# Six tiles between state-space chunks, two of GpSimd's products on ScalarE, and a new order of split weights and attention steps

## What is computed

```python
h = rmsnorm(x, norm_mix_pre[l])
proj = h @ w_in[l]
q_na, k_na, v_na, u_ssm, q_mem = jnp.split(proj, [...], axis=-1)
y_na = neighbourhood_attention(...)          # 8 heads of 128
y_ssm = s5_mixer(u_ssm, ...)                 # complex scan over time, both directions, then gelu and a gate
y_mem = memory_cross_attention(q_mem, mem, mem_norm[l], w_mem_kv[l])   # 4 heads of 128
y = jnp.concatenate([rmsnorm(y_na, ...), rmsnorm(y_ssm, ...), rmsnorm(y_mem, ...)], axis=-1)
x = x + rmsnorm(y @ w_out[l], norm_mix_post[l])
```

```
turns = time * c10 - round(time * c8) + time * c11
```

## Time and profile before

| | |
|---|---|
| median of 3 executions | 2292.43 us (2292.24 to 2294.15) |
| the profiled execution | 2285.35 us, span 2282.8 us |
| mean granted TensorE clock | 0.997 |
| TensorE busy | 2241.6 us, 98% of the span |
| VectorE, ScalarE, GpSimd busy | 1351.2, 1022.7, 120.7 us |

### The profile page before, as it was taken

One profiled execution on the slowest core, in us unless ns is written; L12 is line 12 of the kernel. 1 busy time (PEld: TensorE's weight loads), 2 busy tenths in 40 slices (PEclk: granted clock), 3 DMA queues, 4 the chain that ended last, 5 costly groups with the idle time before them and its releaser, 6 DMA issues.

```text
span 2282.8 us, 32803 instructions
## 1 busy us (share of the span) xinstructions
PE 2241.6 (98%) x13292; PEld 1922.4 (84%) x13292; DVE 1351.2 (59%) x1543; ACT 1022.7 (45%) x1392; POOL 120.7 (5%) x82
## 2 busy tenths in 40 slices
PE   8989999999999999999999999999999999999999
PEld 7878978888888888888888988888888888888887
DVE  6998566565554555454476478757455555445454
ACT  6222465544344444344454467646333344344444
POOL 0674000000000000000000000000000000000000
PEclk9999999999999999999999999999999999999999
DMA  8353435556666655565554433355666665555553
GB/s 319 122 132 128 159 132 210 167 174 187 192 186 194 190 189 197 188 253 189 197 161 141 167 111 94 129 191 162 182 184 184 186 183 198 187 195 191 195 191 111
DMA packets 153352, 402.31 MB, mean 176 GB/s; under 512 B 15264, under 2 KB 30880, under 8 KB 133040
## 3 DMA queue, kind: packets, MB, share of 16 engines
q1 hardware_dynamic: 141952, 394.83, 52.2%
q10 hardware_dynamic: 11312, 6.22, 1.1%
HBM read 398.90 MB, written 2.13 MB: 176 GB/s over the span
## 4 chain that ended last, share of the span: by engine, by line
PE 85%; DVE 4%; ACT 2%; issue 1%; ACTq 0%; DVEq 0%
PE ps L749 20%; PE ps L750 10%; PE ps L787 10%; PE ps L788 10%; PE ps L789 10%; PE ps L989 2%; PE ps L990 2%; PE ps L991 2%; PE ps L624 2%; PE ps L625 2%; PE ps L626 2%; PE ps L616 1%; DVE w_low L2246 1%; PE ps L638 1%; PE ps L639 1%; PE ps L640 1%
## 5 line engine op out<-in xcount | busy, mean ns | idle before, releaser
L2246 DVE TENSOR_TENSOR w_low<-raw_weights,w_high 128x1024 fp32r<-128x1024 f32 (+1 forms) x660 | 777.7, 1219 | 784.0 <-ACT w_high L1473 778.0
L1473 ACT ACTIVATE w_high<-raw_weights 128x1024 fp32r<-128x1024 f32 (+1 forms) x652 | 652.4, 1048 | 800.4 <-PE ps L789 398.5
L749 PE MATMUL ps<-x_split,w_high 128*128 128x512 f32 x2048 | 719.4, 397 | 4.2 <-DVE w_low L2246 2.5
L750 PE MATMUL ps<-x_split,w_low 128*128 128x256 f32 x2048 | 571.6, 279 | 0.0
L749 PEld LDWEIGHTS ps<-x_split,w_high 128*128 128x128 f32 x2048 | 384.4, 188 | 98.4 <-DVE w_low L2246 3.6
L787 PE MATMUL ps<-w_high,x_split 128*128 128x512 f32 x1024 | 398.4, 389 | 0.0
L789 PE MATMUL ps<-w_high,x_split 128*128 128x512 f32 x1024 | 398.4, 389 | 0.0
L788 PE MATMUL ps<-w_low,x_split 128*128 128x512 f32 x1024 | 398.3, 389 | 0.0
L750 PEld LDWEIGHTS ps<-x_split,w_low 128*128 128x128 f32 x2048 | 385.9, 188 | 0.0
L789 PEld LDWEIGHTS ps<-w_high,x_split 128*128 128x128 f32 x1024 | 192.2, 188 | 40.2
L787 PEld LDWEIGHTS ps<-w_high,x_split 128*128 128x128 f32 x1024 | 192.2, 188 | 39.9
(11 more groups left out here) (288 smaller groups left out, 2295.5 us busy)
## 6 DMA issues: line engine op xcount, KB each, us to landing
raw_weights<-in_w_ff SPq DMA_DIRECT2D x128, 1024.0 KB, 5.3
raw_weights<-in_w_up SPq DMA_DIRECT2D x64, 1024.0 KB, 5.6
raw_weights<-in_w_down SPq DMA_DIRECT2D x64, 1024.0 KB, 4.8
raw_weights<-in_w_in SPq DMA_DIRECT2D x62, 1024.0 KB, 5.4
raw_weights<-in_w_out SPq DMA_DIRECT2D x32, 1024.0 KB, 4.9
raw_weights<-in_w_mem_kv SPq DMA_DIRECT2D x7, 1024.0 KB, 14.7
residual<-in_xT SPq DMA_DIRECT2D x2, 2048.0 KB, 14.1
region<-t_table ACTq DMA_DIRECT2D x1, 3072.0 KB, 16.3
```

The lines of the kernel that those rows point to most:

```text
L749: nc.tensor.matmul(o, wh[:, q, w], xs[:, kt], start=(kt == 0), stop=False, skip_group_check=True)
L750: last = nc.tensor.matmul(o[:, 0:S], wl[:, q, w], xh[:, kt], start=False, stop=(kt == KT - 1), skip_group_check=True)
L1473: nc.scalar.activation(split_slot(wh_t, k)[:, r], ring_slot(n)[:, r], ACT.Copy).then_inc(rounded, 1)
L2246: V.tensor_tensor(split_slot(wl_t, k)[:, r], ring_slot(n)[:, r], split_slot(wh_t, k)[:, r].bitcast(f32), ALU.subtract).then_inc(split_read ...
```

## The change

Two columns of products move from GpSimd to ScalarE: `angles(i)` writes time * c8 and time * c11 of chunk i with eight activations of 128 by 128 elements into two pairs of buffers in the `scratch` area (the second buffer of the low parts), and GpSimd keeps five instructions. The chunks stand six tiles apart on TensorE, the last two output products stand in q1, the split of the first q1 slots is woven into VectorE's last chunk, and all attention steps up to unit 10 stand four tiles apart.

```diff
-        PERIOD = 5
+        PERIOD = 6
         BU_AFTER = {2 + PERIOD * i: i for i in range(CHUNKS)}
-        Y_AFTER = {10 + PERIOD * i: i for i in range(CHUNKS)}
-        UNITS_AFTER = {**{67 + 4 * i: i for i in range(7)}, 98: 7, 102: 8, 105: 9, 108: 10}
-        GLU_AFTER, SSM_SUM_AFTER, MEM_SUM_AFTER = 79, 99, 101
+        Y_AFTER = {**{11 + PERIOD * i: i for i in range(CHUNKS - 2)}, 49: CHUNKS - 2, 58: CHUNKS - 1}
+        UNITS_AFTER = {70 + 4 * i: i for i in range(11)}
+        GLU_AFTER, SSM_SUM_AFTER, MEM_SUM_AFTER = 79, 98, 103
...
+            def angles(i):
+                if i >= 2:
+                    act.wait_ge(pool_done, at("turns", i - 2))
+                for part, k in zip(angle[i % 2], (8, 11)):
+                    for j in range(4):
+                        m.did(nc.scalar.activation(part[:, j], iota[:, 0:S:2], ACT.Copy, scale=ssm[k][:, 4 * i + j:4 * i + j + 1]), "angles", i)
...
             tables(2)
+            angles(4)
             na_loads()
             decays(2)
...
             round_slot("q1", 3)
             round_slot("k1", 0)
+            act.wait_ge(dve_done, at("gelu_in"))
+            m.did(nc.scalar.activation(gb, gb, ACT.Tanh, scale=0.7978845608028654), "gelu_tanh")
             act.wait_ge(pool_done, at("na_masked"))
             evac("q1", q1[:, 4:8])
             round_slot("k1", 1)
...
+                whole, fine = angle[i % 2]
+                pool.wait_ge(act_done, at("angles", i))
+                m.did(nc.gpsimd.tensor_scalar(whole, whole, MAGIC, MAGIC, ALU.add, ALU.subtract))
                 if i:
                     pool.wait_ge(act_done, at("turned_in", i - 1))
-                m.did(nc.gpsimd.tensor_tensor(tmpb, time, col(8), ALU.mult))
-                m.did(nc.gpsimd.tensor_scalar(tmpb, tmpb, MAGIC, MAGIC, ALU.add, ALU.subtract))
                 m.did(nc.gpsimd.tensor_tensor(turns, time, col(10), ALU.mult))
-                m.did(nc.gpsimd.tensor_tensor(turns, turns, tmpb, ALU.subtract))
-                m.did(nc.gpsimd.tensor_tensor(tmpb, time, col(11), ALU.mult))
-                m.did(nc.gpsimd.tensor_tensor(turns, turns, tmpb, ALU.add))
+                m.did(nc.gpsimd.tensor_tensor(turns, turns, whole, ALU.subtract))
+                m.did(nc.gpsimd.tensor_tensor(turns, turns, fine, ALU.add))
```

More of the change, by code:

```diff
@@ L190, in program @@
         ga, gb, gc = R(17152, 4), R(10496, 4), region[:, 11520:11524].unsqueeze(2)
-        decay, tmpb, turns = tiles(mix_t, 0, 4, HT), tiles(mix_t, 1024, 4, HT), tiles(mix_t, 3072, 4, HT)
+        decay, turns = tiles(mix_t, 0, 4, HT), tiles(mix_t, 3072, 4, HT)
         decay_f = mix_t[:, 0:4 * HT]
+        angle = [tuple(tiles(scratch, 6144 + 1024 * b + 512 * i, 4, HT) for i in range(2)) for b in range(2)]
         same_step = mix_t[:, 2048 - 256:2048].rearrange("p (i c) -> p i c", c=32)
@@ L1765, in _ @@
             tables(0)
+            angles(2)
             evac("u", ut)
@@ L1771, in _ @@
             tables(1)
+            angles(3)
             decays(1)
             tables(2)
+            angles(4)
             na_loads()
@@ L1776, in _ @@
             tables(3)
+            angles(5)
             evac("q0", q1[:, 0:4])
@@ L1788, in _ @@
             x_rounded(1)
+            round_slot("q1", 0)
             decays(7)
-            round_slot("q1", 0)
             act.wait_ge(pe_done, at("bu", CHUNKS - 1))
+            round_slot("q1", 1)
             x_rounded(2)
             x_rounded(3)
-            round_slot("q1", 1)
             evac("qm", qm)
-            act.wait_ge(dve_done, at("gelu_in"))
-            m.did(nc.scalar.activation(gb, gb, ACT.Tanh, scale=0.7978845608028654), "gelu_tanh")
             round_slot("q1", 2)
@@ L1849, in _ @@
             attend1(11)
+            root("memn", 1, 1)
             attend1(12)
@@ L2610, in yev, with x_lower @@
                     tt(o, yp[:, ::-1], o, ALU.add, "yev", i)
+            def x_lower(c):
+                dve.wait_ge(act_done, at("x", "high", c))
+                dve.wait_ge(pe_done, at("slot", SLOT0["qm"] + c))
+                tt(x_low[:, 4 * c:4 * c + 4], xn[:, 4 * c:4 * c + 4], x_high[:, 4 * c:4 * c + 4].bitcast(f32), ALU.subtract, "x", "low", c)
             flat = lambda a: a.rearrange("p t s -> p (t s)")
@@ L2614, in _ @@
             for i in range(CHUNKS):
+                if i == CHUNKS - 1:
+                    x_lower(0)
+                    low("q1", 0)
                 cs, sn = cosb[i % 2], sinb[i % 2]
@@ L2699, in _ @@
             low("v1", 2)
-            moment("memn", 1, 512, ps[:, 3, 0:S])
             attend1(8)
+            part_full("outn", "wout1", 0, 0, "ssmn", "out")
             low("v1", 3)
-            part_full("outn", "wout1", 0, 0, "ssmn", "out")
             attend1(9)
             part_low("outn", "wout1", 0)
+            moment("memn", 1, 512, ps[:, 3, 0:S])
             low("wout1", 0)
```

72 lines of the change are left out of this document (33 added, 39 removed).

## The result

The changed kernel took 2277.05 us, the median of 6 runs (2270.93 to 2279.26), against 2292.76 us (6 runs, 2289.55 to 2294.15) before: a ratio of 0.9926, 95% interval 0.9912 to 0.9939. The forecast was 2278.7 us. Its profiled execution took 2279.26 us, with a span of 2277.5 us.

What follows compares the result with a forecast made beforehand. TensorE bounds the kernel, so only its waits and low-clock time can go: 10.9 (chunks) + 4.7 (attention) - 0.2 (k1) - 1.7 (v1 copy) = 13.7 us; 2292.4 - 13.7 = 2278.7 us, range 2273 to 2287.

Steps and rivals of the forecast that it cites:

- What bounds the kernel: Whole kernel: TensorE, busy 2241.6 of 2282.8 us; only its waiting or lower-clock time can be given back.
- Six tiles: Chunks: TensorE's period becomes 14.18 us against VectorE's 12.85; 7.9 us of waits and 3.0 us of clock loss go.
- the clock's share: Low-clock windows in chunks and attention: 3.0 and 1.7 us counted as lost time that would be regained.
- The products on ScalarE: Chunks: eight activations fit ScalarE's idle time at no cost; VectorE's work falls from 14.01 to 12.85 us per chunk.
- 12 to 13.5 us that the prediction named as a sign: VectorE's work per chunk expected in the changed kernel's profile, with idle time in front, waiting for TensorE.
- one of its rivals: Chunks: GpSimd's five instructions stretch VectorE as before, but six tiles alone remove the waits, also 2279; no separate chance.
- The decays of chunk 2: ScalarE, behind the transfers: up to 3.2 us later, ready near 134 us, with nothing reaching TensorE.
- q1 and the woven split: Start of q1: begins near 204 us, slot 2's low part ready near 216.5, 1.5 us before it is needed.
- second k1 slot: k1: its low part ready about when TensorE asks, near 238 us; 0.2 us charged, bounds nothing and 2 us.
- Attention: Attention steps and v1: four-tile spacing and moved roots and squares remove 0.8 + 2.2 + 1.7 = 4.7 us.
- The new wait: First half slot of wout1: TensorE waits for ScalarE's copy of v1; 1.7 us charged, between 1.2 and 3.3.
- The slower rival: Chunks: ScalarE becomes the bound, reached at 1.4 us per activation; 2297 us and more, chance 0.05.

Runs made afterwards that it cites:

- before once more: The kernel before, unchanged, profiled a second time; its measured stretch from u to wout1 was 303.85 us, against 304.30 us in the first execution.
- e2: The kernel before with only the two products moved to ScalarE, five tiles per chunk, old weave and attention order; 2284.91 us, ratio 0.9968 to before.
- e1: The changed kernel with all seven instructions per chunk back on GpSimd; six tiles, weave and attention order stay; 2277.90 us, ratio 0.9941 to before.
- e5: The changed kernel without the weave: input quarters and q1 slots split behind chunk 7, chunk 6's output product two tiles earlier; 2285.40 us, ratio 0.9975 to before.
- e3: The changed kernel with the attention steps, roots and squares in the order of the kernel before; 2279.48 us, ratio 0.9944 to before.
- e6: The changed kernel with attention step 10 behind tile 109 instead of 110; 2277.41 us, ratio 0.9948 to before.
- e9: The changed kernel with step 10 behind tile 109 and, on VectorE, the reciprocal for memn behind step 10; 2276.33 us, ratio 0.9936 to before.
- e8: The changed kernel with each of the eight activations per chunk made four times, same values; 2290.19 us, ratio 1.0000 to before.
- e10: The kernel before with the two products on ScalarE and chunk 2's decays ahead of chunk 4's angles and the 17 transfers; 2289.82 us, 1 run.

## Why the prediction was right, step by step

**What bounds the kernel.** Right. TensorE makes the same 13292 matmuls, and what the stretch gained is time in which it waited, 10.09 us, and busy time, 5.36 us, nearly all of which the dips account for. (Over the whole execution its busy time rose from 2241.6 to 2244.9 us, for a reason behind the stretch, told below.)

**Six tiles.** Right, and, with the weave that lets q1 start early, the whole of the state-space gain. The 7.9 us of waits went, and the four dips too. The prediction counted 0.17, 0.13 and 0.17 of a window; the one from 180 us (0.96) was left out, and with it the clock's share is 5.1 us in place of 4.7. The sum by its way of counting: 7.9 + 2.2 + 0.8 + 5.1 - 0.85 = 15.15 us, against 10.09 + 5.36 = 15.45 in the stretch. Of the clock's share 1.4 us is luck of the execution: before once more had so much less of it. The forecast had 13.7. The new table also puts one tile more between a chunk's input product and its output product. No run moves that tile alone; by its length, 1.78 us, it could not have held off VectorE's backlog for long, since chunks of 14.01 us would still have fallen behind by 1.6 us each against 12.40.

**The products on ScalarE.** The prediction costed the activations at nothing, and that was right: line 1720 takes 2.50 us for eight, 0.31 us each. By the estimate from the Trainium skill (ScalarE: Activation LUTs, What ACT_TABLE_LOAD costs, where these figures stand, and not in the section that the prediction names), 0.29 us, the trace agrees within 8%. VectorE's work per chunk was taken as 12.85 us, in proportion to GpSimd's instructions. In the quieter chunks it measures 12.0 us where VectorE has no pause (e2) and 10.8 to 11.0 us where it has (the changed kernel), below the 12 to 13.5 us that the prediction named as a sign. What the estimate missed is that the load is not even: one chunk takes 15.87 us, the one beside which GpSimd works through, on the last turns and then on the bias additions, which the change does not touch. (Before, the two chunks beside these took 14.84 and 13.72 us, so that the additions are a worse neighbour than the turns is not shown.) TensorE did not notice, but only just: the output product of chunk 5 needs VectorE's products of chunk 6 that read PSUM, which end at 187.88 + 1.29 = 189.17 us, and it starts at 189.34 us. In e1, with seven instructions on GpSimd, the same place has 0.7 us to spare (188.46 and 189.18 us). That the gain does not need the move, which the prediction gave in passing as "2279 as well" under one of its rivals, is what e1 found: 2277.9 us. So this part of the change was credited with a gain for VectorE that is real (e2: 5.30 us with five tiles) and that six tiles leave without a use. The Trainium skill (SBUF — State Buffer, Who interferes with whom) states that a VectorE instruction with two SBUF inputs and a GpSimd instruction that reads SBUF hold one another off; the trace agrees in kind, with scans of 4.32 us beside GpSimd's additions and 2.34 us alone.

**The decays of chunk 2.** Predicted near 134 us, measured at 128.97 us. The transfers began 3.0 us earlier than before (112.98 against 116.00 us) and took 1.0 us longer, and the eight activations did not come on top of them: the trace has ScalarE executing them while it issues the first five, 113.52 to 116.05 us.

```profile
113.34 0.70 ACTq L1769 DMA_DIRECT2D residual<-in_na_rpb  x1
113.52 0.71 ACT L1720 ACTIVATE scratch<-region,rinv 128x128 f32<-128x128 f32 x2
```

**q1 and the woven split.** q1 began at 203.19 us (forecast 204), and the low part of slot 2 was ready at 215.27 us (forecast 216.5). The 0.2 us charged for the second k1 slot was not needed: no product of q1 or k1 waits. e5 gives the weave its price, 7.6 us.

**Attention.** 4.7 us were forecast as gone, and they are gone in the profiled pair. The new wait was charged at 1.7 us and is 0.85 us. This term was mis-sized, and the measured wait lies under the lower bound of 1.2 us. With T for the end of step 10 on TensorE, 324.70 us, the exponentials begin at 326.60, T + 1.9, as forecast (T + 1.84), so the 0.5 us added for a late VectorE were not needed; and TensorE reaches the banks at 327.80, T + 3.1 and not T + 2.7. Part of the reason behind the term was wrong too: the prediction had it that TensorE never asked for the banks because step 10 stood behind tile 108. e3 puts it back there, and TensorE waits 1.2 us. What had hidden the copy was the half clock behind the wait of 2.2 us, with 0.13 us to spare. Removing the half clock alone would have won some 0.3 us by an estimate from e3 (1.56 us of half clock less the 1.2 us of the wait that it hid), since it brings the copy's wait to light. Step 10 as placed in the changed kernel is as good as one tile earlier (e6), until VectorE's queue is cleared too (e9).

**The slower rival.** ScalarE's bound was put at 1.4 us per activation in each chunk. e8 is at 1.25 us per activation and most chunks hold, which agrees; no run goes over the bound. But the first place to give way is ahead of the chunks, where three sets of activations stand before the copy of u. Extra work in a loop must be priced at the loop's start as well.

**The one execution of the profile.** The profiled executions differ by 6.1 us only (2285.35 and 2279.26), though the stretch gained 15.45. Most of the rest, 8.0 us, was given back in the first up product, which the change does not touch: it lasts from 445.30 to 806.53 us before, 361.23 us, and from 429.57 to 798.79 us, 369.22 us, in the changed kernel. The granted clock is 0.83 from 450 to 460 us in the changed kernel and 1.00 in the whole of the product before, which is up to 1.7 us by the way of counting above; the other 6 us are a pace. Groups of TensorE in 470 to 800 us (count | busy, mean ns), before and changed kernel:

```profile
L749 PE MATMUL ps<-x_split,w_high 128*128 128x512 f32 x949 | 329.2, 393 | 0.0
```

```profile
L750 PE MATMUL ps<-x_split,w_high 128*128 128x512 f32 x926 | 327.4, 399 | 0.0
```

330 us hold 949 of these at the one pace and 931 at the other (e3, whose product fills the window too); the 1024 of a whole product take some 7 us more at the slower one by this count (the second products of before and e3, 368.74 and 362.40 us long, differ by 6.3 us). The medians of this pair (15.7 us apart) agree with the stretch. The prediction carried the difference between the profiled execution and the median over as a constant; that it was this pace was not known.

## What to carry to other kernels

When two engines run a loop in step and the one that bounds the kernel waits, first look whether its other work can be spaced so that the pair fits: here one more tile per chunk, with the split woven in, gave all that taking work off the other engine gave, and more. A dip of the clock may be hiding a wait, so what it costs is not all to be had. For effects under 0.2%, measure between two fixed instructions of the trace, and leave the rest of the program's variation out.

## What the runs showed of the hardware

- The up product's matmuls have two paces, 393 or 394 and 277 ns, or 399 and 281 ns, at a granted clock of 1.00. The pace holds for a whole product and changes from one product or execution to another, whatever the kernel. Before had the first product fast and the second slow, before once more both slow, e3 the first slow and the second fast (394 ns; its span of 2270.9 us is the shortest of the profiled ones), e5 the first fast. The cause is open.
- The same wait of 2.22 us in front of the same transposes was followed by half clock in four executions of the order of before (before twice, e2, e10) and by full clock in one (e3).
- ScalarE executes activations that stand ahead of transfers in its program while it already issues these: eight of 0.31 us lay beside the first five of 17 transfers. Twelve more transfers then took 12.79 us.
